# Turning the non-rotary queries on VectorE instead of TensorE in a fused encoder layer

## The chip, the cores and the metric

The kernel runs on one core of a Trainium2 chip. The time is device microseconds of the whole program, the median of the runs shown. TensorE multiplies and transposes into PSUM; ScalarE, VectorE and GpSimd do the rest; SyncE issues most of the loads. Each engine runs its own instructions in order, and they wait for one another on semaphores.

## The reference

One layer of a streaming encoder on 256 tokens of 2048 channels, in float32. What matters here is the first of its parts, latent attention with 16 heads. `h` is the normed input.

```python
c_q, c_kv, k_rope, u_in, gate_a, gate_b = jnp.split(h @ w_in[l], split_at, axis=-1)
q = (rms_norm(c_q, norm_cq) @ w_uq).reshape(B, S, MLA_HEADS, QK_NOPE + QK_ROPE)   # 128 + 64
q = jnp.concatenate([q[..., :QK_NOPE], apply_rope(q[..., QK_NOPE:], cos, sin)], axis=-1)
kv = (rms_norm(c_kv, norm_ckv) @ w_ukv).reshape(B, S, MLA_HEADS, QK_NOPE + V_HEAD)
s = jnp.einsum('bqhd,bkhd->bhqk', q[:, q0:kend], k[:, :kend]).astype(jnp.float32) * scale
p = jax.nn.softmax(jnp.where(mask, s, NEG_INF), axis=-1).astype(v.dtype)
outs.append(jnp.einsum('bhqk,bkhd->bqhd', p, v[:, :kend]))
```

Beside it stand a convolution branch (GLU, a causal depthwise convolution of 31 taps over 1024 channels, LayerNorm, swish, a pointwise product), a gated merge with `w_o`, cross attention to 256 memory tokens, and a SwiGLU feed-forward layer of width 5632.

## The kernel before

**Weight tiles.** Every weight matrix goes through the same pipeline of 592 tiles in a ring of 4 slots. SyncE loads tile n into `raw` (L289) once VectorE has split tile n-4. ScalarE rounds it to `w_hi` (`split_hi`, L809) once TensorE is through with tile n-4. VectorE takes the rest, `w_lo` (`split_lo`, L1311). TensorE multiplies each tile in three passes, lo x hi, hi x lo and hi x hi (`products`, L365 to L367), 12 matmuls of 512 columns for a full tile. Both splitting engines work four tiles ahead: in their slot t of an iteration they split tile t+4, and then do whatever else is written in that slot.

**Pairs.** The heads are taken two at a time, 8 pairs, one loop iteration each (`gate_and_pair`), 12 tiles long: 8 tiles of a gate chunk from `w_in`, 2 of `w_uq` (the pair's queries, two heads x 192 columns), 2 of `w_ukv` (keys and values). The first iteration, the next ones and the last are written out with small differences; the middle ones are the same code. ScalarE writes the queries to `q_tok` in slot 9, [token, block, head, 192], and keys and values in slot 10. GpSimd turns the 64 rotary columns by their angle and writes `qr_tok`.

**Attention, one iteration later.** In iteration i the attention of pair i-1 is woven between the gate tiles. TensorE, behind tile 1: `queries_turned` transposes `q_tok` (4 blocks, bank 0 of `tp`) and `qr_tok` (2 blocks, bank 1), through `turn_group` (L377); `probs_turn` transposes the probabilities of pair i-2 (L488). ScalarE copies these to `qnT`, `qrT` and `probsT` (L961, L963, L970). Behind tile 3: `values` (L497, L499, pair i-2) and `scores` (L513 rotary part, L518 the rest, pair i-1). VectorE masks the scores in slot 3 (L1452, L1457), ScalarE takes the exponentials in slot 4, and VectorE the gated values and the inverse sums in slot 7. The last pair's attention runs in the first chunk of the memory's keys (the tail, `T_E`), where VectorE also makes the low part of an operand in slots 0 to 4 (`operand_lo`, L1499; one of them in slot 11 of the last iteration).

**Convolution.** VectorE does the depthwise convolution of channel block i in iteration i, 20 of 31 taps (`taps`, L1440 for the first, L1443 for the others; each reads what the one before it wrote, and waits for it on `conv_step`). The lists `share`, `share_first` and `share_last` say how many taps are done by the start of each slot. The other 11 taps of each block follow in the chunks of the memory's keys (`late_taps`).

**Squares.** VectorE's transpose works on blocks of 32 x 32. To turn 128 x 128 blocks it takes 16 instructions, each on 32 partitions, and writes square (i, j) to partitions 32j. The kernel does so already elsewhere (`square_turns`, L1390, 32 x 256 elements each).

Of the kernel before, what the change touches and what calls it, by code (L numbers as in the profile page):

```python
# [23 lines left out]
ACT = mybir.ActivationFunctionType  # L24
# [64 lines left out]
def program(nc, x, memT, positions, vecs, w_in, w_uq, w_ukv, w_dwT, w_pw2, b_pw2, w_o, w_q_mem, w_kv_mem,  # L89
# [10 lines left out]
    with ctx:  # L100
# [127 lines left out]
        kr_ready = sem("kr_ready")  # L228
        kr_step = sem("kr_step")
        g_ready, u_turned, u_ready, tanh_done = (sem(n) for n in ("g_ready", "u_turned", "u_ready", "tanh_done"))  # L230
        q_ready, kv_ready = sem("q_ready"), sem("kv_ready")
        rope_step, rope_ready = sem("rope_step"), sem("rope_ready")
        ckv_scaled = sem("ckv_scaled")
        scores_ready, scores_read = sem("scores_ready"), sem("scores_read")
# [111 lines left out]
        def _(pe):  # L346
# [125 lines left out]
                        turn_group(Q_CKV, 1, [qr_tok[:, b, :, :].rearrange("p h d -> p (h d)") for b in range(NB)])  # L472


            def queries_turned(p, q):

                pe.wait_ge(q_ready, 2 * p + 2)
                turn_group(q, 0, [q_tok[:, b, h, 0:NOPE] for h in range(2) for b in range(NB)])
                pe.wait_ge(rope_ready, p + 1)
                turn_group(q, 1, [qr_tok[:, b, :, :].rearrange("p h d -> p (h d)") for b in range(NB)])  # L480

            def probs_turn(p):

# [19 lines left out]
            def scores(p, q, first):  # L503

                operand_ready(q)
                pe.wait_ge(kv_ready, 2 * p + 2)
                if not first:
                    pe.wait_ge(probs_out, p)
                blocks = ((0, P, 0), (P, TOK, P))
                for qs, keys, at in blocks:  # L510
                    for h in range(2):
                        rows = slice(h * ROPE, (h + 1) * ROPE)
                        mm(sc[:, h, at:at + keys], qrT[rows, qs:qs + P], krT[rows, 0:keys],  # L513
                           start=qs == 0, stop=False, skip_group_check=True)
                for h in range(2):
                    for qs, keys, at in blocks:

                        ins = mm(sc[:, h, at:at + keys], qnT[:, h, qs:qs + P], knT[:, h, 0:keys],  # L518
                                 start=False, stop=True, skip_group_check=True)
                    ins.then_inc(scores_ready, 1)  # L520

            def attention(t, i, nth, parity):

                if t == 1:
                    queries_turned(i - 1, i + (Q_C - 1))
                    if nth > 1:
                        probs_turn(i - 2)
                if t == 3:
                    if nth > 1:
                        values(i - 2, v_pair[parity], nth == 2)  # L530
                    scores(i - 1, i + (Q_C - 1), nth == 1)
# [268 lines left out]
        def _(act):  # L800
# [152 lines left out]
                            fn(sqT[:, 2 * g:2 * g + 2, :], mem_k[:, 2 * g:2 * g + 2, :], ACT.Square).then_inc(sq_done, 1)  # L953


            def queries_out(p, q, first):

                act.wait_ge(turned, 2 * q + 1)
                if not first:
                    act.wait_ge(scores_ready, 2 * p)  # L960
                fn(qnT[:, :, :].rearrange("p h t -> p (h t)"), tp[:, 0, :], ACT.Copy).then_inc(turned_out[0], 1)  # L961
                act.wait_ge(turned, 2 * q + 2)
                fn(qrT[:, :], tp[:, 1, 0:TOK], ACT.Copy).then_inc(turned_out[1], 1)  # L963

            def probs_evicted(p, first):

# [14 lines left out]
            def attention(t, i, nth):  # L981

                if t == 1:
                    queries_out(i - 1, i + (Q_C - 1), nth == 1)
                    if nth > 1:
                        probs_evicted(i - 2, nth == 2)
                if t == 4:
                    exponentials(i - 1)

            def operand_hi(g):  # L990
# [6 lines left out]
            def gate_and_pair(i, nth, parity=0, last=False):  # L997
                first = nth == 0
                for t in range(12):
                    if t == 7:  # L1000
                        if first:
                            act.wait_ge(sq_out, 1)
                        for b in range(NB):
                            acc_full(b, i * 3 + C_C, i * 12 + (T_C + 8))
                            fn(gates[:, b, cols(i * CH, CH)], acc[:, b, :], ACT.Tanh, scale=half_rx[:, b:b + 1])\
                                .then_inc(acc_free[b], 1)
                    if t == 9:

                        if not first:
                            act.wait_ge(turned, 2 * i + (2 * Q_C - 1))  # L1010
                            act.wait_ge(rope_ready, i)
                        for b in range(NB):
                            acc_full(b, i * 3 + (C_C + 1), i * 12 + (T_C + 10))
                            fn(q_tok[:, b, :, :].rearrange("p h d -> p (h d)"), acc[:, b, 0:UQ], ACT.Copy,
                               scale=rfac[:, R_CQ, b:b + 1]).then_inc(q_ready, 1)
                            act.wait_ge(q_ready, 2 * i + (b + 1))
                            act.sem_inc(acc_free[b], 1)
                    if t == 10:
                        if not first:
                            act.wait_ge(scores_ready, 2 * i)  # L1020
                        if nth > 1:
                            act.wait_ge(pv_done, i - 1)
                        for b, dst in enumerate((knT[:, :, :].rearrange("p h t -> p (h t)"),
                                                 v_pair[parity][:, :, :, :].rearrange("p b h d -> p (b h d)"))):
                            acc_full(b, i * 3 + (C_C + 2), i * 12 + (T_C + 12))
                            fn(dst, acc[:, b, :], ACT.Copy).then_inc(kv_ready, 1)
                            act.wait_ge(kv_ready, 2 * i + (b + 1))
                            act.sem_inc(acc_free[b], 1)
                    width = {8: 2 * UQ, 9: 2 * UQ, 10: CH, 11: CH}.get(t + 4, TW)
                    split_hi(i * 12 + T_C, t + 4, width)  # L1030
                    if first and t == 2:
                        act.wait_ge(g_ready, 1)
                        sigmoid_turned(1, Q_B)
                    if first and t < 2:
                        operand_hi(t)
                    if last and t == 11:
                        act.wait_ge(tile_done, i * 12 + (T_C + 8))
                        operand_hi(2)
                    if not first:
                        attention(t, i, nth)  # L1040
# [262 lines left out]
        def _(dve):  # L1303
# [126 lines left out]
                        u_turn(t, c - 1)  # L1430


            def taps(j, w0, w1, before):

                for w in range(w0, w1):
                    u = uT[:, cols(j, 1), w:w + TOK].rearrange("p o t -> p (o t)")
                    a = conv[:, cols(j, 1), :].rearrange("p o t -> p (o t)")
                    wt = wdwT[:, cols(j, 1), w:w + 1].rearrange("p o t -> p (o t)")
                    if w == 0:
                        ins = V.tensor_scalar(a, u, wt, vcol("b_dw", j), ALU.mult, ALU.add)  # L1440
                    else:
                        dve.wait_ge(conv_step, before + (w - w0))
                        ins = V.scalar_tensor_tensor(out=a, in0=u, scalar=wt, in1=a, op0=ALU.mult, op1=ALU.add)  # L1443
                    ins.then_inc(conv_step, 1)

            def masked_scores(p, first):

# [32 lines left out]

            def attention(t, i, nth):

                if t == 3:
                    masked_scores(i - 1, nth == 1)
                if t == 7:
                    if nth > 1:
                        gate_values(i - 2)
                    row_inverse(i - 1, nth == 1)

            share = [0, 0, 2, 3, 4, 6, 8, 10, 12, 14, 16, 18, EARLY_TAPS]  # L1490
            share_first = [0, 0, 0, 0, 0, 6, 8, 10, 12, 14, 16, 18, EARLY_TAPS]
            share_last = [0, 3, 6, 7, 9, 12, 15, 18, 18, 18, 19, 19, EARLY_TAPS]

            def operand_lo(g):

# [18 lines left out]
            def gate_and_pair(i, nth, last=False):  # L1514
                first = nth == 0
                for t in range(12):
# [21 lines left out]
                    if not first:  # L1538
                        attention(t, i, nth)
                    at = share_first if first else share_last if last else share  # L1540
                    if at[t + 1] > at[t]:
                        taps(i, at[t], at[t + 1], i * EARLY_TAPS + at[t])

            gate_and_pair(0, 0)
            gate_and_pair(1, 1)
# [5 lines left out]
            LATE = TAPS - EARLY_TAPS  # L1551
            after_c = CT * EARLY_TAPS

            def late_taps(c, t, at=(0, 3, 6, 9, 12, 15, 18, 21, 22)):

                order = [(half, EARLY_TAPS + w) for half in range(2) for w in range(LATE)]
                for n in range(at[t], at[t + 1]):
                    half, w = order[n]
                    taps(c * 2 + half, w, w + 1, c * (2 * LATE) + (after_c + n))

            for t in range(8):
                split_lo(T_E, t + 4)
                if t < 5:
                    operand_lo(t + 3)
                attention(t, PAIRS, PAIRS)
                late_taps(0, t, (0, 0, 1, 3, 6, 10, 14, 18, 22))
            for t in range(8):
                split_lo(T_E + 8, t + 4)
                if t == 7:
# [486 lines left out]
```

## Time and profile before

| | |
|---|---|
| median of 3 runs | 1660.77 us (1660.75 to 1664.26) |
| the profiled execution | 1661.55 us |
| its span, first to last instruction | 1659.7 us |
| TensorE busy | 1649.0 us, 99% |
| VectorE busy | 1128.0 us, 68% |
| ScalarE busy | 822.1 us, 50% |
| GpSimd busy | 109.4 us, 7% |

Busy time is a mean over stages of different kinds. Matmuls overlap, so the distance between two starts says what one costs (0.23 us for 512 columns), not its duration of 0.39 us. The same holds for VectorE where one instruction starts before the one ahead has ended. The pairs take about 34.0 us each and end at 403.58 us, where the tail begins.

### The profile page before, as it was taken

To read this page: it belongs to the slowest core of one execution; us is meant where nothing else is said; L and a number is where in the kernel's file an instruction comes from. 1 tells how busy PE (TensorE), PEld (TensorE's weight loads), DVE (VectorE), ACT (ScalarE), POOL (GpSimd) and SP (SyncE) were. 2 spreads that over 40 slices of the span, in tenths; PEclk is the share of its full clock that TensorE was granted. 3 is DMA by queue.
4 is the path that set the end of the run, shared out by engine and by line. 5 is a ranking of instruction groups with operands and counts; after the bars stand their busy time and mean duration, and the time that the engine had idled before them with its cause. 6 is when DMAs were issued, how large, how long until landed. Compare 5 with 4: busy or idle time off the path is not lost.

```text
span 1659.7 us, 23379 instructions
## 1 busy us (share of the span) xinstructions
PE 1649.0 (99%) x7760; PEld 1379.9 (83%) x7760; DVE 1128.0 (68%) x1461; ACT 822.1 (50%) x1050; POOL 109.4 (7%) x154
## 2 busy tenths in 40 slices
PE   9999999999999999999999999999999999999997
PEld 8888888888888888888888888888888888888886
DVE  5678777778986466986568856666666666654453
ACT  7556545555546444566555544444444444344343
POOL 3100111120000000120001200000000000000000
PEclk9999999999999999999999999999999999999999
DMA  6875655556565665564446666666666666665564
GB/s 232 252 206 169 179 161 148 169 159 186 174 213 183 195 208 178 192 195 157 141 127 201 198 195 191 191 195 194 190 188 185 196 202 192 194 221 180 185 214 133
DMA packets 161114, 309.78 MB, mean 187 GB/s; under 512 B 10240, under 2 KB 16896, under 8 KB 160800
## 3 DMA queue, kind: packets, MB, share of 16 engines
q1 hardware_dynamic: 158864, 301.50, 59.1%
q0 software_dynamic: 1488, 6.42, 1.1%
q10 hardware_dynamic: 704, 1.11, 0.2%
q8 instruction: 34, 0.56, 0.1%
q14 instruction: 24, 0.20, 0.0%
HBM read 306.89 MB, written 2.10 MB: 186 GB/s over the span
## 4 chain that ended last, share of the span: by engine, by line
PE 97%; DMA 1%; ACT 1%; issue 1%; DVE 0%; SPq 0%; POOLq 0%; POOL 0%; ACTq 0%; DVEq 0%
PE acc L365 30%; PE acc L367 29%; PE acc L366 29%; PE tp L377 1%; DMA raw<-in_w_in_dram 1%; PE sc L518 1%; PE acc L594 1%; PE acc L596 1%; PE acc L595 1%; PE ov L499 0%; PE sc L513 0%; PE sc L488 0%; PE acc L565 0%; ACT w_hi L809 0%; PE acc L576 0%
## 5 line engine op out<-in xcount | busy, mean ns | idle before, releaser
L1311 DVE TENSOR_TENSOR w_lo<-raw,w_hi 128x1024 fp32r<-128x1024 f32 (+3 forms) x591 | 719.4, 1223 | 415.1 <-ACT w_hi L809 408.4
L809 ACT ACTIVATE w_hi<-raw 128x1024 fp32r<-128x1024 f32 (+3 forms) x591 | 605.7, 1027 | 752.8 <-PE acc L367 715.9
L365 PE MATMUL acc<-w_hi,crossT 128*128 128x512 f32 x832 | 324.8, 390 | 0.1
L366 PE MATMUL acc<-w_lo,crossT 128*128 128x512 f32 x832 | 323.9, 389 | 0.0
L367 PE MATMUL acc<-w_hi,crossT 128*128 128x512 f32 x832 | 323.8, 389 | 0.0
L365 PE MATMUL acc<-w_hi,mixT 128*128 128x512 f32 x732 | 289.3, 395 | 0.8 <-ACTq L904 0.6
L367 PE MATMUL acc<-w_hi,mixT 128*128 128x512 f32 x732 | 285.2, 390 | 0.0
L366 PE MATMUL acc<-w_lo,mixT 128*128 128x512 f32 x732 | 285.1, 389 | 0.0
L365 PEld LDWEIGHTS acc<-w_hi,crossT 128*128 128x128 f32 x832 | 156.2, 188 | 33.0 <-ACTq L1060 0.5
L367 PEld LDWEIGHTS acc<-w_hi,crossT 128*128 128x128 f32 x832 | 156.2, 188 | 32.7
L366 PEld LDWEIGHTS acc<-w_lo,crossT 128*128 128x128 f32 x832 | 156.3, 188 | 31.7
L365 PEld LDWEIGHTS acc<-w_hi,mixT 128*128 128x128 f32 x732 | 137.5, 188 | 30.1 <-DVE w_lo L1311 0.8
L367 PEld LDWEIGHTS acc<-w_hi,mixT 128*128 128x128 f32 x732 | 137.4, 188 | 29.2
L366 PEld LDWEIGHTS acc<-w_lo,mixT 128*128 128x128 f32 x732 | 137.6, 188 | 27.4
L365 PE MATMUL acc<-w_hi,actT 128*128 128x512 f32 x336 | 130.7, 389 | 0.0
L366 PE MATMUL acc<-w_lo,actT 128*128 128x512 f32 x336 | 130.7, 389 | 0.0
L367 PE MATMUL acc<-w_hi,actT 128*128 128x512 f32 x336 | 130.7, 389 | 0.0
L1443 DVE SCALAR_TENSOR_TENSOR conv<-uT,wdwT,conv (+1 forms) x240 | 119.1, 496 | 16.0 <-DVE conv L1443 12.5
L1800 DVE STREAM_TRANSPOSE row_bc<-stage 32x256 f32<-32x256 f32 x176 | 76.7, 436 | 3.6
L366 PEld LDWEIGHTS acc<-w_lo,actT 128*128 128x128 f32 x336 | 63.1, 188 | 13.2
L365 PEld LDWEIGHTS acc<-w_hi,actT 128*128 128x128 f32 x336 | 63.1, 188 | 13.0
L367 PEld LDWEIGHTS acc<-w_hi,actT 128*128 128x128 f32 x336 | 63.1, 188 | 13.0
(273 smaller groups left out, 1555.9 us busy)
## 6 DMA issues: line engine op xcount, KB each, us to landing
raw<-in_w_in_dram SPq DMA_DIRECT2D x104, 512.0 KB, 3.9
raw<-in_w_gate_dram SPq DMA_DIRECT2D x88, 512.0 KB, 4.2
raw<-in_w_up_dram SPq DMA_DIRECT2D x88, 512.0 KB, 3.7
raw<-in_w_down_dram SPq DMA_DIRECT2D x80, 512.0 KB, 4.7
raw<-in_w_kv_mem_dram SPq DMA_DIRECT2D x64, 512.0 KB, 3.8
raw<-in_w_o_dram SPq DMA_DIRECT2D x32, 512.0 KB, 4.4
raw<-in_w_q_mem_dram SPq DMA_DIRECT2D x32, 512.0 KB, 3.8
raw<-in_w_o_mem_dram SPq DMA_DIRECT2D x32, 512.0 KB, 3.8
```

The lines of the kernel that those rows point to most:

```text
L365: mm(o, lo, whi, start=first and k == 0, stop=False)
L366: mm(o, hi, wlo, start=False, stop=False)
L367: ins = mm(o, hi, whi, start=False, stop=end)
L377: ins = turn(tp[:, bank, j * P:(j + 1) * P], src, ident[:, :])
L518: ins = mm(sc[:, h, at:at + keys], qnT[:, h, qs:qs + P], knT[:, h, 0:keys], start=False, stop=True, skip_group_check=True)
L594: mm(o, lo, w_hi[:, s, k * n:(k + 1) * n], start=first and k == 0, stop=False)
L595: mm(o, hi, w_lo[:, s, k * n:(k + 1) * n], start=False, stop=False)
L596: ins = mm(o, hi, w_hi[:, s, k * n:(k + 1) * n], start=False, stop=last and k == kt - 1)
L809: fn(w_hi[:, s, 0:width], raw[:, s, 0:width], ACT.Copy).then_inc(hi_done, 1)
L1311: V.tensor_tensor(w_lo[:, s, 0:width], raw[:, s, 0:width], w_hi[:, s, 0:width].bitcast(F32), ALU.subtract).then_inc(lo_done, 1)
L1443: ins = V.scalar_tensor_tensor(out=a, in0=u, scalar=wt, in1=a, op0=ALU.mult, op1=ALU.add)
L1800: ins = V.transpose(dst[:, :, :, 32 * i:32 * i + 32], src[:, :, :, 32 * j:32 * j + 32])
```

## The change

TensorE no longer transposes `q_tok`. VectorE does, in 16 squares of 32 partitions x 128 elements (`query_turn`), straight to `qnT`. Squares 0 to 3 of a pair go into slots 10 and 11 of its own iteration, squares 4 to 15 into slots 0 to 4 of the next, one behind each convolution tap, and what is left over behind the last tap of the slot. The taps are dealt out anew over the slots. The two rotary blocks are transposed into a bank each. Values and scores come behind tile 5 where they came behind tile 3, the masked scores in slot 5 where they were in slot 3, the exponentials in slot 6 where they were in slot 4. TensorE waits for `q_turned` before the scores. ScalarE no longer copies `qnT`, and waits for `q_turned` before it overwrites `q_tok`.

```diff
--- before.py
+++ after.py
@@ -228,7 +228,7 @@
         kr_ready = sem("kr_ready")
         kr_step = sem("kr_step")
         g_ready, u_turned, u_ready, tanh_done = (sem(n) for n in ("g_ready", "u_turned", "u_ready", "tanh_done"))
-        q_ready, kv_ready = sem("q_ready"), sem("kv_ready")
+        q_ready, q_turned, kv_ready = sem("q_ready"), sem("q_turned"), sem("kv_ready")
         rope_step, rope_ready = sem("rope_step"), sem("rope_ready")
         ckv_scaled = sem("ckv_scaled")
         scores_ready, scores_read = sem("scores_ready"), sem("scores_read")
@@ -472,12 +472,11 @@
                         turn_group(Q_CKV, 1, [qr_tok[:, b, :, :].rearrange("p h d -> p (h d)") for b in range(NB)])
 
 
-            def queries_turned(p, q):
-
-                pe.wait_ge(q_ready, 2 * p + 2)
-                turn_group(q, 0, [q_tok[:, b, h, 0:NOPE] for h in range(2) for b in range(NB)])
+            def rotary_turned(p, q):
+
                 pe.wait_ge(rope_ready, p + 1)
-                turn_group(q, 1, [qr_tok[:, b, :, :].rearrange("p h d -> p (h d)") for b in range(NB)])
+                for b in range(NB):
+                    turn_group(q, b, [qr_tok[:, b, :, :].rearrange("p h d -> p (h d)")])
 
             def probs_turn(p):
 
@@ -503,6 +502,7 @@
             def scores(p, q, first):
 
                 operand_ready(q)
+                pe.wait_ge(q_turned, p + 1)
                 pe.wait_ge(kv_ready, 2 * p + 2)
                 if not first:
                     pe.wait_ge(probs_out, p)
@@ -522,10 +522,10 @@
             def attention(t, i, nth, parity):
 
                 if t == 1:
-                    queries_turned(i - 1, i + (Q_C - 1))
+                    rotary_turned(i - 1, i + (Q_C - 1))
                     if nth > 1:
                         probs_turn(i - 2)
-                if t == 3:
+                if t == 5:
                     if nth > 1:
                         values(i - 2, v_pair[parity], nth == 2)
                     scores(i - 1, i + (Q_C - 1), nth == 1)
@@ -953,14 +953,13 @@
                             fn(sqT[:, 2 * g:2 * g + 2, :], mem_k[:, 2 * g:2 * g + 2, :], ACT.Square).then_inc(sq_done, 1)
 
 
-            def queries_out(p, q, first):
-
-                act.wait_ge(turned, 2 * q + 1)
+            def rotary_out(p, q, first):
+
                 if not first:
                     act.wait_ge(scores_ready, 2 * p)
-                fn(qnT[:, :, :].rearrange("p h t -> p (h t)"), tp[:, 0, :], ACT.Copy).then_inc(turned_out[0], 1)
-                act.wait_ge(turned, 2 * q + 2)
-                fn(qrT[:, :], tp[:, 1, 0:TOK], ACT.Copy).then_inc(turned_out[1], 1)
+                for b in range(NB):
+                    act.wait_ge(turned, 2 * q + (b + 1))
+                    fn(qrT[:, b * P:(b + 1) * P], tp[:, b, 0:P], ACT.Copy).then_inc(turned_out[b], 1)
 
             def probs_evicted(p, first):
 
@@ -981,10 +980,10 @@
             def attention(t, i, nth):
 
                 if t == 1:
-                    queries_out(i - 1, i + (Q_C - 1), nth == 1)
+                    rotary_out(i - 1, i + (Q_C - 1), nth == 1)
                     if nth > 1:
                         probs_evicted(i - 2, nth == 2)
-                if t == 4:
+                if t == 6:
                     exponentials(i - 1)
 
             def operand_hi(g):
@@ -1007,7 +1006,7 @@
                     if t == 9:
 
                         if not first:
-                            act.wait_ge(turned, 2 * i + (2 * Q_C - 1))
+                            act.wait_ge(q_turned, i)
                             act.wait_ge(rope_ready, i)
                         for b in range(NB):
                             acc_full(b, i * 3 + (C_C + 1), i * 12 + (T_C + 10))
@@ -1430,8 +1429,18 @@
                         u_turn(t, c - 1)
 
 
-            def taps(j, w0, w1, before):
-
+            def query_turn(n):
+
+                i, j = n // 4, n % 4
+                src = q_tok[32 * i:32 * i + 32, :, :, 32 * j:32 * j + 32]
+                to = qnT[32 * j:32 * j + 32, :, :].rearrange("p h (b t) -> p b h t", b=NB)
+                ins = V.transpose(to[:, :, :, 32 * i:32 * i + 32], src)
+                if n == 15:
+                    ins.then_inc(q_turned, 1)
+
+            def taps(j, w0, w1, before, turns=()):
+
+                turns = list(turns)
                 for w in range(w0, w1):
                     u = uT[:, cols(j, 1), w:w + TOK].rearrange("p o t -> p (o t)")
                     a = conv[:, cols(j, 1), :].rearrange("p o t -> p (o t)")
@@ -1442,6 +1451,10 @@
                         dve.wait_ge(conv_step, before + (w - w0))
                         ins = V.scalar_tensor_tensor(out=a, in0=u, scalar=wt, in1=a, op0=ALU.mult, op1=ALU.add)
                     ins.then_inc(conv_step, 1)
+                    if turns:
+                        query_turn(turns.pop(0))
+                for n in turns:
+                    query_turn(n)
 
             def masked_scores(p, first):
 
@@ -1480,16 +1493,18 @@
 
             def attention(t, i, nth):
 
-                if t == 3:
+                if t == 5:
                     masked_scores(i - 1, nth == 1)
                 if t == 7:
                     if nth > 1:
                         gate_values(i - 2)
                     row_inverse(i - 1, nth == 1)
 
-            share = [0, 0, 2, 3, 4, 6, 8, 10, 12, 14, 16, 18, EARLY_TAPS]
+            share = [0, 2, 4, 6, 8, 10, 10, 12, 12, 14, 16, 18, EARLY_TAPS]
             share_first = [0, 0, 0, 0, 0, 6, 8, 10, 12, 14, 16, 18, EARLY_TAPS]
-            share_last = [0, 3, 6, 7, 9, 12, 15, 18, 18, 18, 19, 19, EARLY_TAPS]
+            share_last = [0, 2, 5, 7, 9, 11, 11, 14, 14, 15, 16, 18, EARLY_TAPS]
+            turn_now = {0: (4, 6), 1: (6, 9), 2: (9, 11), 3: (11, 13), 4: (13, 16)}
+            turn_next = {10: (0, 2), 11: (2, 4)}
 
             def operand_lo(g):
 
@@ -1538,8 +1553,13 @@
                     if not first:
                         attention(t, i, nth)
                     at = share_first if first else share_last if last else share
+                    turns = range(*turn_next.get(t, (0, 0)) if first or t > 9 else turn_now.get(t, (0, 0)))
+                    if t == 10:
+                        dve.wait_ge(q_ready, 2 * i + 2)
+                        if not first:
+                            dve.wait_ge(scores_ready, 2 * i)
                     if at[t + 1] > at[t]:
-                        taps(i, at[t], at[t + 1], i * EARLY_TAPS + at[t])
+                        taps(i, at[t], at[t + 1], i * EARLY_TAPS + at[t], turns)
 
             gate_and_pair(0, 0)
             gate_and_pair(1, 1)
@@ -1551,19 +1571,24 @@
             LATE = TAPS - EARLY_TAPS
             after_c = CT * EARLY_TAPS
 
-            def late_taps(c, t, at=(0, 3, 6, 9, 12, 15, 18, 21, 22)):
+            def late_taps(c, t, at=(0, 3, 6, 9, 12, 15, 18, 21, 22), turns=()):
+
+                turns = list(turns)
 
                 order = [(half, EARLY_TAPS + w) for half in range(2) for w in range(LATE)]
                 for n in range(at[t], at[t + 1]):
                     half, w = order[n]
-                    taps(c * 2 + half, w, w + 1, c * (2 * LATE) + (after_c + n))
+                    taps(c * 2 + half, w, w + 1, c * (2 * LATE) + (after_c + n), turns[:1])
+                    turns = turns[1:]
+                for n in turns:
+                    query_turn(n)
 
             for t in range(8):
                 split_lo(T_E, t + 4)
                 if t < 5:
                     operand_lo(t + 3)
                 attention(t, PAIRS, PAIRS)
-                late_taps(0, t, (0, 0, 1, 3, 6, 10, 14, 18, 22))
+                late_taps(0, t, (0, 2, 4, 6, 8, 11, 12, 17, 22), range(*turn_now.get(t, (0, 0))))
             for t in range(8):
                 split_lo(T_E + 8, t + 4)
                 if t == 7:
```

## Rows read from the trace of the kernel before

**Rows 1.** The page: TensorE's busy time, and the chain that ended last by engine.
```profile
PE 1649.0 (99%) x7760; PEld 1379.9 (83%) x7760; DVE 1128.0 (68%) x1461; ACT 822.1 (50%) x1050; POOL 109.4 (7%) x154
...
PE 97%; DMA 1%; ACT 1%; issue 1%; DVE 0%; SPq 0%; POOLq 0%; POOL 0%; ACTq 0%; DVEq 0%
```

**Rows 2.** TensorE's waits: who for whom, us in total, times, longest.
```profile
PE acc L365 <- DVE w_lo L1311: 0.2, 1, 0.2
```

**Rows 3.** Busy time by stretch, one iteration: length, engines, granted clock, DMA.
```profile
301.50:335.50 34.00, 34.00 (x186) 29.43 (x185) 25.80 (x41) 17.99 (x29) 5.20 (x7) 1.00 0.55 162
```

**Rows 4.** Timeline of TensorE: start us, us, engine, line, operation, operands, count.
```profile
301.53 0.40 PE L365 MATMUL acc<-w_hi,mixT 128*128 128x512 f32 x1
...
306.99 0.60 PE L377 MATMUL tp<-ident,q_tok 128*128 128x128 f32 x4
307.43 0.38 PE L377 MATMUL tp<-ident,qr_tok 128*128 128x128 f32 x2
307.64 0.82 PE L488 MATMUL sc<-ident,probs 128*128 128x128 f32 x6
308.22 0.48 PE L365 MATMUL acc<-w_hi,mixT 128*128 128x512 f32 x1
...
313.80 0.38 PE L497 MATMUL ov<-v_odd,probsT 128*128 128x128 f32 x2
...
315.23 0.93 PE L513 MATMUL sc<-krT,qrT 64*128 64x128 f32 x8
...
335.55 0.40 PE L365 MATMUL acc<-w_hi,mixT 128*128 128x512 f32 x1
```

**Rows 5.** Timeline of VectorE, slots 9, 10, 11 and 4.
```profile
335.83 1.49 DVE L1311 TENSOR_TENSOR w_lo<-raw,w_hi 128x1024 fp32r<-128x1024 f32 x1
...
338.51 1.49 DVE L1311 TENSOR_TENSOR w_lo<-raw,w_hi 128x1024 fp32r<-128x1024 f32 x1
339.92 0.47 DVE L1443 SCALAR_TENSOR_TENSOR conv<-uT,wdwT,conv  x1
340.57 0.48 DVE L1443 SCALAR_TENSOR_TENSOR conv<-uT,wdwT,conv  x1 [0.18 <-DVE conv L1443]
340.97 1.22 DVE L1311 TENSOR_TENSOR w_lo<-raw,w_hi 128x1024 fp32r<-128x1024 f32 x1
342.11 0.48 DVE L1443 SCALAR_TENSOR_TENSOR conv<-uT,wdwT,conv  x1
...
355.34 0.96 DVE L1311 TENSOR_TENSOR w_lo<-raw,w_hi 128x768 fp32r<-128x768 f32 x1 [1.16 <-ACT w_hi L809]
356.22 0.48 DVE L1443 SCALAR_TENSOR_TENSOR conv<-uT,wdwT,conv  x1
356.87 0.48 DVE L1443 SCALAR_TENSOR_TENSOR conv<-uT,wdwT,conv  x1 [0.18 <-DVE conv L1443]
```

**Rows 6.** Timeline of ScalarE, the split for slot 9.
```profile
333.63 1.06 ACT L809 ACTIVATE w_hi<-raw 128x1024 fp32r<-128x1024 f32 x1 [0.18 <-ACT q_tok L1014]
```

**Rows 7.** Squares elsewhere: VectorE's timeline, and its groups by form.
```profile
105.91 1.23 DVE L1311 TENSOR_TENSOR w_lo<-raw,w_hi 128x1024 fp32r<-128x1024 f32 x1
107.17 1.33 DVE L1390 STREAM_TRANSPOSE conv<-stage 32x256 f32<-32x256 f32 x3
...
L1390 DVE STREAM_TRANSPOSE uT<-stage 32x256 f32<-32x256 f32 x32 | 13.9, 436 | 0.6
```

**Rows 8.** Timeline of VectorE and TensorE around the start of the tail.
```profile
402.68 1.28 DVE L1311 TENSOR_TENSOR w_lo<-raw,w_hi 128x1024 fp32r<-128x1024 f32 x1 [1.32 <-ACT w_hi L809]
...
403.58 0.40 PE L365 MATMUL acc<-w_hi,row_r 128*128 128x512 f32 x1
...
403.88 0.69 DVE L1443 SCALAR_TENSOR_TENSOR conv<-uT,wdwT,conv 128x256 f32<-128x256 f32 x1
...
407.93 0.88 DVE L1499 SCALAR_TENSOR_TENSOR mixT<-xs,vecT,mixT 128x256 fp32r<-128x256 f32 x2
```

**Rows 9.** Loads between 160 and 440 us: KB each, median us to landing.
```profile
raw<-in_w_in_dram SPq DMA_DIRECT2D x54, 512.0 KB, 3.6
```

## The prediction

> **What bounds the kernel now.** I read the page's busy shares first, then the chain that ended last: TensorE is busy 99% of the span and 97% of the chain is TensorE [rows 1]. The waits of TensorE come next. For weight tiles they hold 0.2 us in all [rows 2]. So every instruction taken from TensorE pays in full, and every new wait on TensorE costs in full. VectorE has room only on average: 25.8 of the 34.0 us of one pair's iteration [rows 3]. The question is whether it has room between the two points that the change ties together, so I laid the timelines of both engines over one iteration [rows 4 to 6].
>
> In an iteration (start 301.53, next start 335.55) TensorE meets tiles 0 and 1, the transposes, tiles 2 and 3, the values and the scores, then tiles 4 to 11. VectorE handles tile t+4 in its slot t, so its slots 9, 10 and 11 belong to the next iteration's tiles 1, 2, 3.
>
> **What goes from TensorE.** Four transposes of q_tok per pair: 306.99 to 307.43, 0.44 us [rows 4]. Eight pairs: 3.5 us. The two rotary transposes and the six of the probabilities stay (0.21 and 0.58). Values and scores move behind tile 5 with their own cost unchanged. ScalarE exchanges one 512-column and one 256-column copy for two of 128 columns, and its exponentials move two slots later. I price both at nothing: it runs 18.0 of 34 us in an iteration [rows 3] and tile 9's split, below, is set by TensorE's end of the tile before and the q_tok copies. The wait before q_tok is rewritten is long met (the squares end in slot 4, the copy is in slot 9).
>
> **What comes to VectorE.** 16 squares of 32 partitions x 128 elements per pair, in slots 10 and 11 (2 each) and, one iteration on, 0 to 4 (2, 3, 2, 2, 3). Taps move too: slots 0 to 4 now have 2 each (before 0, 2, 1, 1, 2), slots 5 and 7 none. The masked scores leave slot 3 for slot 5. The new wait is TensorE's, ahead of the scores: it needs the last square, which stands at the end of slot 4. Queued behind it on TensorE is everything.
>
> *Price of a square.* A square of 256 elements takes 0.436 us [rows 7]. The splits of 768 and 1024 elements take 0.96 and 1.22 [rows 5], 0.26 per 256 elements, so 128 elements fewer save 0.13: 0.30 us, an estimate. Bounds: half of the larger square, 0.22, and all of it, 0.44. *What it hides.* A tap starts 0.65 after the one it depends on but the next independent instruction 0.40 after [rows 5], so a square between two taps could use 0.25 us. But three squares behind a split start 0.03 after the split's end (105.91 + 1.23 = 107.14, next at 107.17), and take 1.33, so they don't overlap at all [rows 7], where a tap starts 1.14 into a split of 1.22 [rows 5]. I take the squares as not overlapping: tap 0.48 + 0.03, square 0.30, together 0.81, and the third square of a slot 0.30. If they did overlap, tap and square would be 0.70.
>
> The Trainium skill says the same in its page VectorE: DVE Perf Modes, section "Two Vector instructions with no wait between them": an instruction is held until all earlier ones are finished when its input or output starts in another quadrant of partitions than the last one's. By that rule 15 of the 16 squares are held, and so is the tap behind each; rows 7 agree. With the hold a slot of two taps and two squares is 2.76, without it 2.54, and the eight lateness terms below would each be about 1.5 smaller.
>
> *The chain, a middle iteration.* Slot 9 begins when ScalarE's split of tile 13 ends, 333.63 + 1.06 = 334.69 [rows 6], plus 0.04, which is 0.82 before the next iteration's start 335.55. (It began at 335.83 because slot 7's taps, now gone, delayed it.) Slot by slot, starts to starts:
> slot 9: 2.68 (335.83 to 338.51);
> slot 10: 1.41 (338.51 to 339.92) + 2 x 0.81 = 3.03;
> slot 11: 1.14 + 1.62 = 2.76;
> slot 0: 2.76; slot 1: 2.76 + 0.30 = 3.06; slots 2 and 3: 2.76 each;
> slot 4: 0.88 (355.34 to 356.22) + 1.62 + 0.30 = 2.80.
> Sum 22.61, and no slot has to wait for its tile (slot 4 begins at 19.0 of the iteration, its tile is free at about 15.6). The last square ends at 22.61 - 0.82 = 21.79.
> TensorE's arrival at the scores: tiles 0 and 1, 5.46; transposes 1.23 - 0.44 = 0.79; tiles 2 and 3, 5.58 (308.22 to 313.80); tiles 4 and 5, 2 x 2.72; values 1.43 (313.80 to 315.23) [rows 4]. Sum 18.70. **TensorE waits 3.1 us in each middle iteration.** The start of the chain hangs on tiles behind the scores of the iteration before, so the wait does not shrink from one to the next.
>
> *All eight.* Iteration 1 has neither values nor transposes of probabilities: arrival 2.01 earlier, wait 5.1. Iterations 2 to 6: 5 x 3.1 = 15.5. Iteration 7 has a third tap in slot 1: 3.6. The eighth pair's scores lie in the first chunk of the memory keys: slots 11 and 0 to 4 also carry two operand instructions each (at 407.93: 0.88, of which 0.08 overlaps with the next), 6 x 0.80 = 4.8; slot 4's split is of 1024 elements (+0.26), slot 9 has one tap fewer (403.88 + 0.60 - 402.68 = 1.80 for 2.68), its start is 0.90 before 403.58 [rows 8]. End 22.61 + 4.80 + 0.26 - 0.88 - 0.90 = 25.9, wait 7.2 (some of it earlier, at tiles 3 to 5, which need those operands). Sum 31.4.
>
> Net 31.4 - 3.5 = +27.9. The profiled execution took 1661.55 us (span 1659.7, 1.85 around it), 0.8 above the median of 1660.77; on the median the forecast is **1688.7**.
>
> Cover elsewhere: the splits that TensorE needs come early enough. The tightest is slot 0's, which ends 8.8 into the iteration where tile 4 starts at 11.8. Its slot then loads again by 12.4 (3.6 us is a load's time in this stretch [rows 9]), before it is wanted at about 14.6. The later late-taps (5 in each of slots 6 and 7 of the tail) end about where they ended before.
>
> **Ends.** With squares of 0.22 that overlap: two-and-two slots 1.14 + 0.65 + 0.40 + 0.22 = 2.41, the chain 20.0, a middle wait 0.5, the eight together about 10.5: +7. With 0.44 and held: 16 x 0.13 = 2.1 more each, 17 in all: +45.
>
> **Rivals.**
> 1. *The squares hide, TensorE doesn't wait* (the other side). The wait vanishes when slots 9 to 4 take at most 19.5 us for my 22.6; then only the 3.5 us are left: 1657.3. For it: 8 us of idle VectorE in an iteration, and 0.25 us free behind each tap. Against: the idle time lies in slots 3 to 8, not in these; before the change, with four taps fewer in slots 0 to 4 and no square, slot 4's taps end at 357.35 [rows 5], 21.8 into the iteration (the masked scores and their maxima in it), and the memory part needs 4.6 even at the low end. The Trainium skill's rule for authors (VectorE: DVE Perf Modes, "Rules for kernel authors") is that VectorE's transpose is the fastest for 32x32 blocks, which would speak for the change; here the four on TensorE take 0.44 us and the sixteen squares by my estimate 4.8. Chance 5%, and 2% that it comes to nothing.
> 2. *Half hidden*: squares overlap (0.70 per tap and square) or cost 0.25. Middle wait 1.6 to 2.3, in all +15 to +21: 1676 to 1682. Chance 18%.
> 3. *The clock falls too.* Waits of 3 to 7 us are longer than any in the trace, whose granted clock is 1.00 [rows 3]. If each let the clock fall from 2.4 to 1.2 GHz for one tile behind it, 2.72 us more each, 22 in all: about 1710. No row here shows a fall. The Trainium skill (TensorE: Matmul & The Clock Gate, Part 1) says an idle TensorE is throttled to half; a fall behind only the two longest waits would give 1694. Chance of 1704 or more, 8%.
> Forecast as told (1682 to 1703): 67%. Range 1673 to 1704, which leaves about 15% outside. A measurement of this kernel can tell about 0.2%, 3.3 us: faster 0.05, same 0.02, slower 0.93.
>
> **What would show it.** After the change: TensorE's waits list a new wait ahead of the first rotary score matmul, released by VectorE's transpose, 8 times, about 3 us, longest 5 to 7; the STREAM_TRANSPOSE rows at 0.30 us each, 128 of them; the tap behind a square starting after the square's end; VectorE without a wait for w_hi from slot 9 to slot 4; iterations of 36.7 us for 34.0; the q_tok transposes gone from TensorE. I am wrong if the squares take 0.2 us or overlap, or if slot 9 starts other than 0.8 before the iteration.

## The result and the profile after

| | before | after |
|---|---|---|
| median | 1660.76 us (1660.46 to 1664.26, 4 runs) | 1709.66 us (1709.32 to 1710.69, 4 runs) |
| profiled execution, span | 1661.55, 1659.7 us | 1709.32, 1707.5 us |
| mean granted clock | 0.999 | 0.991 |

The change costs 2.9% (ratio 1.0291, 95% interval 1.0279 to 1.0303), 48.9 us. The forecast was 1688.7 us and its range ended at 1704. The spans of the two profiled executions differ by 47.8 us, of which the forecast had 27.9.

The page of the kernel after, for [rows 1]: TensorE has 32 matmuls fewer but is busy 11 us longer, and only 88% of the chain that ended last is TensorE, where it was 97%.

```profile
PE 1660.0 (97%) x7728; PEld 1384.5 (81%) x7728; DVE 1167.8 (68%) x1589; ACT 817.4 (48%) x1050; POOL 103.6 (6%) x154
...
PE 88%; DVE 5%; issue 3%; ACT 2%; DMA 1%; DVEq 0%; POOL 0%; POOLq 0%; ACTq 0%; SPq 0%
```

TensorE's waits, for [rows 2]:

```profile
PE sc L513 <- DVE qnT L1437: 19.0, 5, 5.2
PE sc L513 <- issue: 12.4, 3, 5.4
PE acc L594 <- ACT gates L1004: 2.8, 7, 0.5
PE acc L365 <- DVE mixT L1514: 2.2, 4, 0.9
...
```

The two rows of L513 are one wait, for the last of the 16 squares, met 8 times: 31.4 us. "Issue" names no releaser, but its three cases (iterations 2 and 7 and the tail) stand at the same place and end 0.21 us behind the end of the last square; the five that name VectorE end 0.26 to 0.38 behind it. The third row is a wait that the prediction did not have, 7 times, at tile 8, the first behind the moved exponentials. The fourth, 4 times, stands in the tail, at tiles 2 to 5, which need the operands that VectorE makes there.

VectorE's timeline, slots 9, 10, the start of 11, and slot 4, for [rows 5]:

```profile
323.88 1.45 DVE L1310 TENSOR_TENSOR w_lo<-raw,w_hi 128x1024 fp32r<-128x1024 f32 x1 [0.37 <-ACT w_hi L809]
...
326.78 1.23 DVE L1310 TENSOR_TENSOR w_lo<-raw,w_hi 128x1024 fp32r<-128x1024 f32 x1 [0.17 <-ACT w_hi L809]
327.93 0.47 DVE L1452 SCALAR_TENSOR_TENSOR conv<-uT,wdwT,conv  x1
328.32 0.29 DVE L1437 STREAM_TRANSPOSE qnT<-q_tok 32x128 f32<-32x128 f32 x1
328.58 0.48 DVE L1452 SCALAR_TENSOR_TENSOR conv<-uT,wdwT,conv  x1
329.10 0.30 DVE L1437 STREAM_TRANSPOSE qnT<-q_tok 32x128 f32<-32x128 f32 x1
329.41 1.23 DVE L1310 TENSOR_TENSOR w_lo<-raw,w_hi 128x1024 fp32r<-128x1024 f32 x1
...
343.67 0.96 DVE L1310 TENSOR_TENSOR w_lo<-raw,w_hi 128x768 fp32r<-128x768 f32 x1
344.55 0.48 DVE L1452 SCALAR_TENSOR_TENSOR conv<-uT,wdwT,conv  x1
345.06 0.30 DVE L1437 STREAM_TRANSPOSE qnT<-q_tok 32x128 f32<-32x128 f32 x1
345.37 0.48 DVE L1452 SCALAR_TENSOR_TENSOR conv<-uT,wdwT,conv  x1
345.89 0.63 DVE L1437 STREAM_TRANSPOSE qnT<-q_tok 32x128 f32<-32x128 f32 x2
```

Read it against the forecast. Slot 9 starts at 323.88, 0.81 before the iteration's first matmul at 324.69 (forecast 0.82). The last square ends at 346.52, so the chain took 22.64 us (forecast 22.61). The first square of a pair, (0, 0), starts and ends on partitions 0 to 31 like the tap ahead of it. It starts 0.39 behind that tap's start, 0.08 before the tap's end, and the next tap 0.26 behind it. Every other square starts 0.03 after the tap ahead or 0.01 after the square ahead has ended, and the tap behind it 0.01 after the square: 0.82 to 0.83 us for tap and square. In brackets stand two waits of VectorE for ScalarE's `w_hi`: the one at slot 9 was in the forecast, as what starts the chain, the one at slot 10 was not. It takes 0.17 to 0.30 us in the iterations and 1.08 in the tail. All 128 squares:

```profile
L1437 DVE STREAM_TRANSPOSE qnT<-q_tok x128: 292/302/308, 170.3 to 466.6; 32x128 f32<-32x128 f32 x128
```

TensorE in the same iteration and in the one before it, for [rows 4]:

```profile
307.73 1.65 PE L513 MATMUL sc<-krT,qrT 64*128 64x128 f32 x8 [3.45 <-DVE qnT L1437]
309.31 2.44 PE L518 MATMUL sc<-knT,qnT 128*128 128x128 f32 x8
...
342.83 0.61 PE L498 MATMUL ov<-v_odd,probsT 128*128 128x128 f32 x4
346.86 0.93 PE L513 MATMUL sc<-krT,qrT 64*128 64x128 f32 x8 [3.43 <-DVE qnT L1437]
347.72 1.58 PE L518 MATMUL sc<-knT,qnT 128*128 128x128 f32 x8
348.95 0.58 PE L365 MATMUL acc<-w_hi,mixT 128*128 128x512 f32 x1
...
355.10 0.44 PE L594 MATMUL acc<-w_hi,cqT 128*128 128x384 f32 x1 [0.33 <-ACT gates L1004]
```

The same 16 score matmuls take 2.1 us from start to start at 346.86 and 3.7 at 307.73. The waits ahead of them differ by 0.02 us. What differs is the clock. Busy time by stretch (length; TensorE, its loads, VectorE, ScalarE, GpSimd; granted clock; DMA share; GB/s):

```profile
265.00:268.50 3.50, 0.10 (x1) 0.01 (x1) 3.35 (x8) 0.33 (x1) 0.00 (x0) 1.00 0.43 112
268.50:271.00 2.50, 2.48 (x16) 2.02 (x17) 0.66 (x1) 0.00 (x0) 0.00 (x0) 0.83 0.68 181
343.40:346.80 3.40, 0.04 (x1) 0.00 (x0) 3.26 (x8) 0.35 (x1) 0.00 (x0) 1.00 0.49 105
346.80:349.00 2.20, 2.14 (x17) 1.76 (x17) 0.71 (x1) 0.00 (x0) 0.00 (x0) 1.00 0.69 202
190.00:193.00 3.00, 3.00 (x11) 2.43 (x10) 0.00 (x0) 0.00 (x0) 0.00 (x0) 0.50 0.62 175
```

TensorE idles 3.4 us and the clock is then 0.83 in the mean over 2.5 us in one iteration, and 1.00 in another; behind the 5.2 us of iteration 1 it is 0.50, which is 1.2 GHz. It fell behind six of the eight waits, all but those of iterations 5 and 6.

The whole difference, from distances between starts on TensorE in both traces:

| | us |
|---|---|
| waits ahead of the scores: 5.26, 3.26, 3.49, 3.53, 3.49, 3.51, 3.88 and, in the tail, 5.46 with 3.4 behind it at tiles 2 to 5 | +35.2 |
| score matmuls at a low clock: 1.87, 1.61, 0.44, 1.57, 0, 0, 0.67, 1.87 | +8.0 |
| tiles behind them at a low clock | +3.6 |
| waits and slow first matmuls at tile 8 (7 times 0.5 to 0.7) and at the same place in the tail (1.2) | +5.3 |
| four transposes fewer, eight times | -3.5 |
| iteration 1 starts 0.76 earlier | -0.8 |
| sum | +47.8 |

The scores and the tiles behind them taken together, each of the six falls cost 1.6 to 3.0 us, 11.6 in all.

### The profile page after: what moved, and what is told of

It reads as the page before. It is cut to its first block, busy times and chain, and to the rows that moved or that the text cites. A ratio compares the mean times of both kernels' runs of the same rounds, so it can differ in the third digit from the quotient of the medians.

```text
span 1707.5 us, 23443 instructions
## 1 busy us (share of the span) xinstructions
PE 1660.0 (97%) x7728; PEld 1384.5 (81%) x7728; DVE 1167.8 (68%) x1589; ACT 817.4 (48%) x1050; POOL 103.6 (6%) x154
## 4 chain that ended last, share of the span: by engine, by line
PE 88%; DVE 5%; issue 3%; ACT 2%; DMA 1%; DVEq 0%; POOL 0%; POOLq 0%; ACTq 0%; SPq 0%
PE acc L365 27%; PE acc L367 26%; PE acc L366 26%; DVE w_lo L1310 2%; DVE conv L1452 1%; PE tp L377 1%; PE sc L518 1%; DVE qnT L1437 1%; ACT w_hi L809 1%; ACT probs L977 1%; PE acc L594 1%; PE acc L596 1%; PE acc L595 1%; PE sc L513 1%; DMA raw<-in_w_uq_dram 0%
```

## The experiments

Theory A: the 21 us that the forecast lacked are the clock's fall (12), ScalarE's exponentials in their new slot (5) and waits that are longer than worked out (4). Its rival stands in each expectation. The code is shown in part; "+" and "-" are against the kernel after, in kernel 3 against the kernel before. Ratios are to runs of the kernel before on the same chip (1661.0 us beside kernels 1, 2, 3 and 5, 1661.3 beside 4, 6, 7 and 8).

**1. TensorE kept at work while it waits.** Matmuls into a bank that nobody reads fill most of the wait ahead of the scores; nothing else is changed.

```
+ for _ in range(24 if first or isinstance(p, int) and p == PAIRS - 1 else 15):
+     mm(xt[:, 0:P], ident[:, :], ident[:, :], start=True, stop=True)
  pe.wait_ge(q_turned, p + 1)
```

> Ahead of the wait for the squares TensorE does idle matmuls of 128 columns into an unused bank: 15 in a middle iteration (0.21 us each by the 22 at the kernel's start, so 3.1 us of a wait of 3.5), 24 in the first and in the tail. The squares land when they landed, so no wait is taken away. Theory A, the clock falls because TensorE stands still ahead of the scores, and costs 13.3 us: scores and the tiles behind them at full pace in all eight places, granted clock 1.00, time 1709.7 - 11 to 13 = 1697 to 1699. Rival B, the slow scores are a matter of their operands or of VectorE's and ScalarE's traffic beside them, not of the clock: 1709 to 1711.

Measured: 1697.31 us (1697.23 to 1697.42), ratio 1.0217 (1.0200 to 1.0234): 12.35 us less than the change, although TensorE has more to do. TensorE's timeline, and then the stretches of the filled wait and of the scores, of this kernel:

```profile
260.65 3.51 PE L506 MATMUL xt<-ident 128*128 128x128 f32 x30
264.15 0.93 PE L515 MATMUL sc<-krT,qrT 64*128 64x128 f32 x8
265.01 1.58 PE L520 MATMUL sc<-knT,qnT 128*128 128x128 f32 x8
266.23 0.59 PE L365 MATMUL acc<-w_hi,mixT 128*128 128x512 f32 x1
```

```profile
260.60:264.10 3.50, 3.50 (x32) 3.37 (x31) 3.33 (x9) 0.44 (x1) 0.00 (x0) 1.00 0.49 107
264.10:266.20 2.10, 2.10 (x16) 1.68 (x16) 0.76 (x1) 0.00 (x0) 0.00 (x0) 1.00 0.63 205
```

The scores of every pair now take 0.86 and 1.23, as before the change. So the 12 us are, but for some tenths, what the idle time in those waits does to the clock, and A holds for them: by the distances between starts this trace is 11.9 us shorter than that of the change, where the slow matmuls made up 11.6.

**2. The exponentials one slot later.** They stand at the end of ScalarE's slot 6, ahead of its copies of the gates.

```
- if t == 6:
+ if t == 7:
```

> ScalarE's exponentials go from slot 6 to the end of slot 7, behind the evictions of the gate chunk and the split. Theory A: TensorE's wait for the gates' eviction (0.33 to 0.48 us at tile 8, with the slower first matmul 0.5, in seven iterations) comes from the exponentials standing ahead of it on ScalarE, 3.5 us in all: 1706, if the clock falls in the same iterations (the phase may shift it by 3 either way). Rival B: the gates' eviction is late for VectorE's or TensorE's own lateness: the wait stays and the time is 1709 to 1711.

Measured: 1711.93 us (1708.68 to 1713.68), ratio 1.0308 (1.0291 to 1.0325). TensorE's waits of this kernel:

```profile
...
PE acc L565 <- ACTq L1016: 2.5, 7, 0.4
...
```

The wait at the gates is gone from tile 8 and a like one stands at the keys and values, which need a bank that ScalarE must first empty of the queries. That was not foreseen: A expected 1706 and missed, and the rival, whose time is nearer, had the wait stay at the gates. ScalarE's work is displaced, and the wait goes with it. As a test of the price it says nothing; the next kernel does. It shows something else: its waits ahead of the scores are those of the change to 0.07 us, and the clock again fell behind six of eight, but other ones. Behind iterations 2 and 3 the scores took 0.86 and 1.23 us, and behind 5 and 6 they were slowed.

**3. The move alone.** The kernel before, with its transposes on TensorE, and only values, scores, masked scores and exponentials two slots later.

```
- if t == 3:      # values, scores
+ if t == 5:
...
- if t == 4:      # exponentials
+ if t == 6:
...
- if t == 3:      # masked scores
+ if t == 5:
```

> The kernel before, with values, scores, masked scores and exponentials two slots later and nothing else: TensorE still transposes the queries, VectorE has no squares, taps are dealt as before. Theory A, the loss is the wait for the squares and what follows from it: only the 0.5 us at tile 8 in seven iterations is left, 1664 (1662 to 1666). Rival B, the move itself delays VectorE or the splits: 1670 or more.

Measured: 1666.65 us (1666.19 to 1667.73), ratio 1.0033 (1.0021 to 1.0046), 5.6 over the kernel before. TensorE's waits:

```profile
PE acc L594 <- ACT gates L1005: 2.8, 7, 0.5
...
PE acc L365 <- ACTq L1060: 1.0, 1, 1.0
...
```

The same wait, 2.8 us in 7, with no square in the kernel, and the one at L1060 in the tail. They belong to the move alone: by distances between starts tile 8 costs 4.1 us in seven iterations and the same place in the tail 1.2, together the 5.3 of the changed kernel. The cause in the changed kernel, on ScalarE's timeline:

```profile
353.89 0.49 ACT L977 ACTIVATE probs<-probs,negmax 128x256 f32<-128x256 f32 x1
354.29 0.19 ACT L977 ACTIVATION_READ_ACCUMULATOR probs<-probs,negmax 128x1 f32 x1
354.38 1.24 ACT L1004 ACTIVATE gates<-acc,half_rx 128x512 f32 x2
```

The gates' bank is full when the last tile of the chunk ends (start of its last pass 354.38), and tile 8 needs one of the two copies done. Its first matmul comes at 355.10.

**4. Four taps of slots 0 to 4 put elsewhere.** In iterations 1 to 6 six taps instead of ten between the iteration's start and the last square, with three in slot 5 (none before) and three in slot 6 (two before). The last iteration and the tail stay.

```
- share = [0, 2, 4, 6, 8, 10, 10, 12, 12, 14, 16, 18, EARLY_TAPS]
+ share = [0, 1, 2, 3, 4, 6, 9, 12, 12, 14, 16, 18, EARLY_TAPS]
```

> Iterations 1 to 6 have 6 convolution taps in slots 0 to 4 instead of 10 (1, 1, 1, 1, 2) and 3 each in slots 5 and 6; squares, waits, the last iteration and the tail stay. Theory A, the wait is the sum of VectorE's instructions from slot 9 to slot 4: four taps at 0.51 to 0.53 us fewer, so the wait falls by 2.1 in six iterations (12.5 us), and with waits of 1.4 left the clock does not fall in iterations 2 to 6, another 3 to 8: 1690 to 1694. Rival B, a tap beside a square is hidden and costs nothing: no change, 1709.

Measured: 1693.04 us (1692.25 to 1693.82), ratio 1.0187 (1.0170 to 1.0204). TensorE's waits:

```profile
PE sc L513 <- issue: 10.3, 3, 5.4
PE sc L513 <- DVE qnT L1437: 8.7, 5, 3.1
...
```

The waits of iterations 2 to 6 fell from between 3.2 and 3.5 us to 1.10, 1.44, 1.37, 1.36 and 1.40, by 2.0 to 2.1 for four taps, and behind none of the five did the scores slow (0.86 and 1.23 each). Behind the first (3.14), the seventh (3.82) and the last (5.39) they did. That is A's split of a wait: its length, and behind a long one the clock. The limit, if there is a fixed one, is not measured: 1.47 us (kernel 7) had no fall behind it and 3.14 had one, but 3.43 and 3.44 in the changed kernel had none.

**5. Two of sixteen squares.** Fourteen of the sixteen 32 x 32 squares of each 128 x 128 block of the non-rotary queries are left out, so most of those queries are zero in the scores. GpSimd clears `qnT` once at the start.

```
+ if n % 15:
+     return
...
+ G.memset(qnT[:, :, :], 0.0)
```

> Of the 16 squares only the first and the last of a pair are made (the other 14 blocks of the non-rotary queries are left out), the wait and the dealing of the taps stay. Theory A, the wait is the length of VectorE's row of work from slot 9 to slot 4 (22.7 us, TensorE is there after 19.2 of it): without 14 squares it is 18.4, so no wait in the middle iterations, about 1 us in the first, 4.5 in the tail: 1665 to 1671. Rival B, the last square comes late because slot 4 itself comes late, whatever stands in the slots ahead: the wait only falls by the 0.9 us of slot 4's squares, 1695 to 1702.

Measured: 1668.53 us (1667.93 to 1670.39), ratio 1.0046 (1.0029 to 1.0063). Waits ahead of the scores are left at two places:

```profile
PE sc L513 <- issue: 3.3, 1, 3.3
...
PE sc L513 <- DVE qnT L1439: 0.7, 1, 0.7
...
```

5.6 for the move, less 3.5, and 4.0 for these is 6.1 of the 7.5 over the kernel before; the tail's matmuls at a low clock (1.78 for 1.23 in the second half of the scores) are part of the rest. Nearly all that the change costs hangs on the number of squares in the chain, not on the wait as such.

**6. Every square twice.** The first of each two writes a buffer that nobody reads, on the same partitions as the second.

```
+ spare = ln_tok[32 * j:32 * j + 32, 1, 0:2 * TOK].rearrange(...)
+ V.transpose(spare[:, :, :, 32 * i:32 * i + 32], src)
```

> Each square is issued twice, the first time into an unused buffer at the same partitions. Theory A: 0.30 to 0.32 us for each of the 16 more, nothing hides, 4.9 to 5.1 us more at each of the eight waits, 40 us; waits of 8 to 14 us let the clock fall every time, and at about 3.1 us each (as at the first one now) that is 25 for the 12 now: 1709.7 + 40 + 13 = 1763 (1755 to 1768). Rival B, part of a square hides behind the taps' own dependence: 1735 to 1750.

Measured: 1740.52 us (1739.51 to 1741.32), ratio 1.0473 (1.0456 to 1.0491). The theory's 1763, from 0.30 us more for every square, missed; the rival, with squares that overlap in part, held it. VectorE's timeline:

```profile
346.24 0.30 DVE L1438 STREAM_TRANSPOSE ln_tok<-q_tok 32x128 f32<-32x128 f32 x1
346.48 0.26 DVE L1439 STREAM_TRANSPOSE qnT<-q_tok 32x128 f32<-32x128 f32 x1
346.75 1.22 DVE L1310 TENSOR_TENSOR w_lo<-raw,w_hi 128x1024 fp32r<-128x1024 f32 x1
```

The second square starts 0.24 behind the start of the first, while that still runs, and a middle wait rose by 3.0 us (3.43 to 6.44), 0.19 for each of 16. Only the second of two squares with the same partitions overlaps: what serialises the squares of the change is that each starts on other partitions than its neighbour, not that they are transposes. The clock was low behind all eight waits, of 6.3 to 8.3 us (mean 0.981 over the span).

**7. The scores one slot later still, fewer taps ahead of the last square.** Values, scores and masked scores in slot 6, the exponentials in slot 11 (slot 7 in the tail), the inverse sums one iteration later. Slots 3 and 4 have one tap fewer each, slot 5 two more; the last iteration has eight in slots 0 to 4 for eleven, the tail five for eleven.

```
- share = [0, 2, 4, 6, 8, 10, 10, 12, 12, 14, 16, 18, EARLY_TAPS]
+ share = [0, 2, 4, 6, 7, 8, 10, 12, 12, 14, 16, 18, EARLY_TAPS]
...
- if t == 6:      # exponentials
+ if t == (7 if nth == PAIRS else 11):
```

> All eight pairs by squares, but values and scores behind tile 6, masked scores in slot 6, the exponentials at the end of slot 11 (where ScalarE stands idle) and the inverse sums one iteration later; two taps of slots 3 and 4 go to slot 5, and the tail has one tap in each of slots 0 to 4. Theory A (VectorE's row of 21.7 us against an arrival at 21.4, no exponentials ahead of the gates' eviction): no wait and no gate wait in iterations 2 to 7, about 1.5 us in the first and 3.5 in the tail, with a little low clock there: 1662 to 1666. Rival B, the exponentials cost elsewhere again, as they did in slot 7: 1667 or more.

Measured: 1663.37 us (1662.97 to 1665.02, 10 runs), ratio 1.0012 (1.0002 to 1.0021). TensorE's waits:

```profile
...
PE sc L513 <- DVE qnT L1439: 1.5, 1, 1.5
PE acc L365 <- DVE mixT L1516: 1.1, 3, 0.5
PE sc L487 <- ACT probs L979: 0.8, 1, 0.8
...
```

From scores to scores the middle iterations take 33.55 to 33.59 us, 0.43 to 0.47 less than before the change, which is what the four transposes cost (0.44). The ends, where the squares have no room, give it back and 2.0 us more. No scores ran at a low clock.

**8. As 7, with the first and the last pair transposed by TensorE.** The two pairs whose squares TensorE had to wait for go back to the old way, and the taps of the last iteration and the tail are dealt out anew.

```
- rotary_turned(i - 1, i + (Q_C - 1))
+ (queries_turned if nth in (1, PAIRS) else rotary_turned)(i - 1, i + (Q_C - 1))
...
- pe.wait_ge(q_turned, p + 1)
+ if by_dve:
+     pe.wait_ge(q_turned, p)
```

> The same, but the first and the last pair's queries are transposed by TensorE as before the change (their scores come where the row of squares is longest against the arrival): squares for six pairs. Theory A: no wait anywhere, 6 x 0.44 = 2.6 us gained, 1658.4 (1657 to 1661), against 1661.0 before. Rival B, moving the scores costs TensorE or ScalarE something in each iteration: 1663 to 1668.

Measured: 1658.73 us (1657.72 to 1662.07, 10 runs), ratio 0.9984 (0.9974 to 0.9994). All of TensorE's waits:

```profile
PE ov L395 <- POOL ident L1917: 1.5, 1, 1.5
PE acc L365 <- ACTq L912: 1.2, 1, 1.2
PE acc L365 <- DVE w_lo L1332: 0.2, 1, 0.2
```

It is the fastest of the kernels here, by 2.6 us (0.16%), as six pairs at 0.44 us let expect. The interval excludes no change by little.

## Why the prediction was wrong

*Right, and measured so.* That nothing on TensorE could be hidden; that the new wait is TensorE's, ahead of the rotary scores and behind the last square, 8 times; the price of a square (302 ns for an estimated 0.30) and that it is held (0.82 to 0.83 per tap and square for 0.81); the chain (22.64 for 22.61) and its start (0.81 for 0.82), though two small errors cancel in it: slot 10 waits for `w_hi` (0.17), and the first square of a pair is not held; -3.5 for the transposes; the order of the waits, longest in the first iteration and the tail. Rivals 1 and 2, with hidden or half hidden squares, failed on the timeline; kernel 6 shows why they couldn't hold here, and where such squares do overlap. The iteration of 36.7 us took 37.57 where the clock did not fall (324.69 to 362.26): 0.4 more of wait and 0.5 at tile 8.

The Trainium skill (VectorE: DVE Perf Modes, section "Two Vector instructions with no wait between them") says that an instruction is held where its input or output starts in another quadrant than the last one's; the trace agrees in both directions, for the (0, 0) square (starts 0.08 before the tap's end) and the other fifteen (0.01 to 0.03 after the end of what is ahead), and kernel 6 for squares on the same partitions (0.24 from start to start).

*Wrong: the clock was left out of the sum.* It stood in the prediction as rival 3 with a chance of 8%, against "no row here shows a fall". That step failed: between its first and its last matmul the kernel before never let TensorE stand for more than 0.6 us, so its rows could not speak against a fall. A condition that the change itself brings about for the first time cannot be ruled out by its absence before. And at one place the trace of before did show a fall, behind TensorE's last matmul, which ends at 1651.38 (columns as above):

```profile
1651.40:1655.40 4.00, 0.00 (x0) 0.00 (x0) 2.15 (x5) 2.06 (x4) 0.55 (x1) 1.00 0.41 144
1655.40:1659.40 4.00, 0.00 (x0) 0.00 (x0) 0.00 (x0) 0.00 (x0) 0.00 (x0) 0.50 0.75 263
```

TensorE stands, the clock stays at 1.00 for 4.0 us and is then 0.50. For waits that the forecast put at 3 to 7 us that was a reason to price a fall. The clock fell behind six of the eight and cost 11.6 us by the distances, about 12 by kernel 1. The rival's own sum, 22 us at 2.72 each, was too high: a fall cost 1.6 to 3.0 us, and behind two waits there was none. Its total of 1710 came near the measurement by luck: it lacked the next two terms.

The Trainium skill (TensorE: Matmul & The Clock Gate, Part 1) says that an idle TensorE is throttled to half and must work to be released. The trace agrees on both levels (1.00 and 0.50 in the stretches above); at waits of about 3.4 us it shows both outcomes, so for each wait of such a length the sum should have held a share of the fall, not nothing.

*Wrong: "I price both at nothing".* The two slots by which ScalarE's exponentials move put them directly ahead of the copies of the gates, whose bank tile 8 needs. The cover named, ScalarE's 16 us of idle time, was an average over the iteration; at this place there was none. Kernel 3 measures the term by itself: 5.6 us, where the changed kernel's trace gives 5.3.

*Undersized: the waits*, 35.2 for 31.4. From the last square's end to the first matmul it releases pass 0.21 to 0.38 us (346.52 to 346.86 in iteration 5), which the forecast set to nothing: 2.3 in eight. The tail was 8.8 for 7.2: slot 10 waited 1.08 for `w_hi`, and slot 4 has three taps there, where the sum counted the two of a middle iteration (0.5).

Together 11.6 + 5.3 + 3.8 = 20.7, less the 0.8 by which iteration 1 starts earlier: the 19.9 that the spans lie above the forecast (47.8 for 27.9). In the medians it was low by 21.0, since the two profiled executions lie 0.8 above and 0.3 below theirs. What decides which 3.4 us wait lets the clock fall stays open: iterations 4 and 5 have the same instructions and the same wait, and one fell; in kernel 2, with the same waits, both did.

## What to carry to other kernels

Moving work off the bounding engine onto one with idle time on average pays only if the new chain ends before the bounding engine arrives: lay the chain slot by slot first. Here it ended 21.8 us into the iteration, and TensorE arrived at 18.7. Where a wait of some microseconds is then left on TensorE, price it at its length plus a fall of the clock behind it, here 1.6 to 3.0 us at six of eight, or fill it with matmuls that nobody reads, which here gave 12 of 48.9 us back. And when work moves by a slot, ask on each engine what now stands behind it: the exponentials that moved with the scores cost more (5.6 us) than the transposes saved (3.5).

## What the runs showed of the hardware

- The granted clock fell behind six of eight idle stretches of TensorE of 3.18 to 5.39 us, and behind all eight of 6.3 to 8.3 in kernel 6; in kernel 4 it never fell behind 1.10 to 1.44 us, and fell behind 3.14. Matmuls into an unread bank, 0.117 us from start to start, held it.
- Two transposes of 32 x 128 on the same partitions start 0.23 to 0.24 us apart, 0.06 to 0.07 before the first ends (kernel 6); on other partitions 0.32, 0.01 after it (kernel after).
- From the end of VectorE's last square to TensorE's first matmul behind it: 0.21 to 0.38 us in the eight waits of the kernel after.
